# Seven products over a second group of inner tiles, in one more pair of a down projection

## The reference, cut to what matters

```python
D_MODEL = 1024
SEQ = 512
DEPTH = 2
D_FF = ((8 * D_MODEL + 3 * 256 - 1) // (3 * 256)) * 256   # 2816
...
    f = rms_norm(h, ffn_norm)
    gate, up = jnp.split(f @ w_gate_up, 2, axis=-1)
    return h + (jax.nn.silu(gate) * up) @ w_down
```

## Time and profile before

| | |
|---|---|
| median of three runs | 1248.59 us |
| profiled execution, first to last instruction | 1246.9 us |
| TensorE busy (PE) | 1232.7 us, 99% |
| VectorE busy (DVE) | 1025.6 us, 82% |
| ScalarE busy (ACT) | 699.0 us, 56% |
| GpSimd busy (POOL) | 171.2 us, 14% |
| granted TensorE clock, whole span | 1.000 |
| stretch of the down projection's pairs 1 to 3 in layer 1 | 1156.48 us to the last matmuls at about 1243.8 us |

### The profile page before, as it was taken

The page is one execution under the profiler, slowest core; times in us unless marked ns, Lnnn a source line. Parts: engine busy times, 40 slices in busy tenths (PEclk is TensorE's granted clock), DMA queues, the critical chain, the costliest instruction groups (busy, mean ns, idle before and its releaser), DMA issues.

```text
span 1246.9 us, 23723 instructions
## 1 busy us (share of the span) xinstructions
PE 1232.7 (99%) x9336; PEld 1181.9 (95%) x9336; DVE 1025.6 (82%) x1692; ACT 699.0 (56%) x1158; POOL 171.2 (14%) x120
## 2 busy tenths in 40 slices
PE   7999999999999999999999999999999999999999
PEld 7999999999999999999998899988899999998998
DVE  5797789588999999897665888894989999989865
ACT  6675547656555555753355765395665555558332
POOL 2564213100000000000033553121000000000000
PEclk9999999999999999999999999999999999999999
DMA  5322111132322222233323221110422332212333
GB/s 198 103 73 86 52 35 35 35 135 71 133 103 102 102 102 69 85 100 118 105 89 102 92 85 53 52 35 18 135 102 102 129 109 102 102 69 85 119 119 119
DMA packets 27387, 114.01 MB, mean 91 GB/s; under 512 B 3472, under 2 KB 4112, under 8 KB 21904
## 3 DMA queue, kind: packets, MB, share of 16 engines
q1 hardware_dynamic: 26560, 111.45, 26.9%
q10 hardware_dynamic: 720, 1.09, 0.2%
HBM read 108.79 MB, written 2.10 MB: 89 GB/s over the span
## 4 chain that ended last, share of the span: by engine, by line
PE 94%; DVE 3%; ACT 1%; issue 1%; POOL 1%; DMA 0%; SPq 0%; DVEq 0%; ACTq 0%; POOLq 0%
PE ps L1404 22%; PE ps L1410 11%; PE ps L1019 11%; PE ps L1115 6%; PE ps L1121 6%; PE ps L1116 6%; PE ps L1025 5%; PE ps L1488 5%; PE ps L1524 4%; PE ps L1245 3%; PE ps L1493 2%; PE ps L1529 2%; PE ps L1193 2%; PE ps L1218 2%; PE ps L1228 1%
## 5 line engine op out<-in xcount | busy, mean ns | idle before, releaser
L1115 PE MATMUL ps<-xhi,whi 128*128 128x264 f32 (+1 forms) x616 | 174.0, 310 | 1.3 <-DVE feat L2251 1.3
L1116 PE MATMUL ps<-xlo,whi 128*128 128x264 f32 (+1 forms) x616 | 167.5, 300 | 0.0
L888 POOL TENSOR_TENSOR wlo<-raw,whi 128x1024 fp32r<-128x1024 f32 x48 | 119.1, 2483 | 181.6 <-ACT whi L1702 181.0
L1115 PEld LDWEIGHTS ps<-xhi,whi 128*128 128x128 f32 x616 | 116.1, 188 | 5.9 <-DVE feat L2251 1.5
L1116 PEld LDWEIGHTS ps<-xlo,whi 128*128 128x128 f32 x616 | 116.2, 189 | 3.6
L1702 ACT ACTIVATE whi<-raw 128x1024 fp32r<-128x1024 f32 x74 | 77.9, 1054 | 55.0 <-PE ps L1025 30.6
L1121 PE MATMUL ps<-xhi,wlo 128*128 128x264 f32 (+1 forms) x616 | 100.5, 305 | 0.8 <-POOL wlo L888 0.8
L1121 PEld LDWEIGHTS ps<-xhi,wlo 128*128 128x128 f32 x616 | 85.3, 188 | 5.1 <-POOL wlo L888 1.2
L1404 PE MATMUL ps<-fhi,hi_a 128*128 128x264 f32 (+1 forms) x352 | 88.2, 283 | 0.0
L1404 PE MATMUL ps<-flo,hi_a 128*128 128x264 f32 (+1 forms) x352 | 88.1, 282 | 0.0
L1404 PE MATMUL ps<-flo,hi_b 128*128 128x264 f32 (+1 forms) x320 | 80.3, 283 | 0.0
(11 more groups left out here) (376 smaller groups left out, 3871.9 us busy)
## 6 DMA issues: line engine op xcount, KB each, us to landing
raw<-in_weights SPq DMA_DIRECT2D x116, 512.0 KB, 3.5
raw<-in_groups SPq DMA_DIRECT2D x42, 1024.0 KB, 4.8
out_hT<-h SPq DMA_DIRECT2D x7, 256.0 KB, 4.9
h<-in_hT SPq DMA_DIRECT2D x4, 264.0 KB, 6.3
h<-in_hT ACTq DMA_DIRECT2D x4, 264.0 KB, 6.0
cst<-in_consts SPq DMA_DIRECT2D x1, 780.5 KB, 9.0
xnb<-feat SPq DMA_DIRECT2D x10, 66.5 KB, 2.1
feat<-xnb SPq DMA_DIRECT2D x10, 66.5 KB, 2.1
```

The source lines that it names most:

```text
L888: nc.gpsimd.tensor_tensor(wlo[:, b], raw[:, b], whi[:, b].bitcast(F32), ALU.subtract).then_inc(split_done, 1)
L1115: nc.tensor.matmul(o, whi[:, k % 2, n], xhi[:, n, cut], start=(n == 0), stop=False)
L1116: nc.tensor.matmul(o, whi[:, k % 2, n], xlo[:, n, cut], start=False, stop=False)
```

## The change

The table gets pair 1 of layer 1, and VectorE makes the low parts of the second forms earlier in that pair, since they are now read there. Pair 1 of layer 0 stays with one group. The host lays the weights of pair 1 out in the other order of units.

```diff
-DN_TWO = ((2, 3), (2, 3))
+DN_TWO = ((2, 3), (1, 2, 3))
...
                             split_down(v + 2)
                             dn_second_weight_sums(p)
                             split_down(v + 3)
+                            if p == 1:
+                                dn_second_forms_low()
                             for a in range(2):
                                 dn_second_sums_low(p, a)
```

## The result

The changed kernel takes **1254.24 us** (median of five, 1253.17 to 1255.08) against 1248.59 (1248.36 to 1249.31): 5.65 us slower, ratio 1.0043 with a 95% interval of 1.0033 to 1.0054. The forecast was 1252.7. The profiled execution took 1254.38 us, its span is 1252.6 (before: 1246.9), and its mean granted clock 0.997 (before: 1.000).

What follows compares the result with a forecast made beforehand. TensorE was taken to bound the kernel, with no slack in layer 1's down projection. Saved work −0.65 plus waits 4.75 gave +4.1 us on 1248.59: 1252.7 us, range 1251.3 to 1254.5.

Steps and rivals of the forecast that it cites:

- sum_vp starts: VectorE's first weight sum in pair 1, forecast at 1162.60 us, 3.61 us later relative to TensorE than in pair 2.
- 1. first F1, high: First group's F1 high product in pair 1 waits for ScalarE's rounded sums; S 0.35 us, 0.46 with the refill.
- 2. first F1, low: First group's F1 low product in pair 1 waits for VectorE's xhi, ending at 1166.41 us; S 0.94 us.
- 3. unit 3, high: Second group's raw high product in pair 1 waits for unit 3's late load and rounding, 1169.70 us; S 2.33.
- 4. unit 3, low: Second group's raw low product in pair 1 waits for VectorE's split of unit 3, ending 1171.27 us; S 3.43.
- 5. second F1, high: Second group's F1 high product in pair 1 waits for the low second forms, ending 1173.47 us; S 4.68.
- 6. second F1, low: Second group's F1 low product in pair 1: low sums met within 0.1 us, S 4.75, nothing late afterwards.
- The term −0.65: TensorE's matmul work saved in pair 1, 66 units of 256 columns in place of 72: 0.65 us won.
- S: TensorE's accumulated delay in pair 1 against pair 2's timing, through the second group's F1 products; forecast 4.75 us.
- VectorE's lateness: VectorE in pair 1 comes 3.61 us later relative to TensorE than in pair 2, and can't catch up.
- The rival: TensorE falls to its lower clock after the waits in pair 1, adding 1.7 us: 1254.4 us; chance 8%.
- The lag stays: Rival: pair 1's snapshots or units 4 and 5 also come a microsecond late, 1253.7 us; chance 7%.

Runs made afterwards that it cites:

- e7: Changed kernel without the low second forms and the second half of the first group's low forms in layer 1 (timing only): 1249.06 us, ratio 1.0006.
- e5: Changed kernel without the low parts of the second forms in layer 1 (timing only): 1252.24 us, ratio 1.0030 to the kernel before.
- e6: Changed kernel without the second half of the first group's low forms in layer 1 (timing only): 1251.02 us, ratio 1.0019 to the kernel before.
- e3: Changed kernel with pair 1's first weight sums made ahead of the second half of the low forms: 1254.10 us, ratio 1.0043 to the kernel before.
- e9: e3 with TensorE's rests filled by 11 and 7 matmuls that nothing reads: 1251.90 us, ratio 1.0027 to the kernel before.
- e8: Changed kernel with layer 1's low second forms made on VectorE near 1144 us, not in pair 1: 1254.64 us, ratio 1.0041 to the kernel before.
- e2: Changed kernel with 22 matmuls that nothing reads ahead of TensorE's three longest waits of pair 1: 1252.57 us, ratio 1.0031 to the kernel before.
- e1: The changed kernel run again unaltered, as yardstick of its batch: 1252.96 us, ratio 1.0043 to the kernel before.
- e4: Changed kernel with layer 1's low second forms made on GpSimd in place of VectorE: 1255.39 us, ratio 1.0053 to the kernel before.
- e10: e8 with 12 and 6 matmuls that nothing reads filling two of TensorE's rests: 1252.82 us, ratio 1.0035 to the kernel before.

## Why the prediction was right, and where it was not

Times after the pair's first matmul (forecast: less 1156.32; measured: less 1155.67):

| step | forecast | measured |
|---|---|---|
| sum_vp starts | 6.28 | 6.29 |
| 1. first F1, high | 8.73 | 8.83 |
| 2. first F1, low | 10.15 | 10.15 |
| 3. unit 3, high | 13.44 | 13.50 |
| 4. unit 3, low | 15.01 | 15.08 |
| 5. second F1, high | 17.21 | 17.28 |
| 6. second F1, low | 17.81 | 18.30 |
| pair 2 starts | 33.63 | 35.90 |

**The term −0.65, TensorE's own work.** Right. e7 shows it, where pair 1 takes 29.96 us with S of 1.09: 28.87 without.

**VectorE's lateness and the waits, items 1 to 5.** Right within 0.1 us each, in order and by releaser. The method held: take a template from the same trace and move each engine by its own offset. e5, e6 and e7 show that the two blocks of low forms carry 3.5 of the 4.64 us, e3 and e9 that the load of unit 3 is worth only the 0.56 us that VectorE rests for it and a little more, and e8 that the place of the second forms is worth nothing (S 4.70 without the clock): the sum of VectorE's work ahead of the second products is what counts.

**Item 6 and the rest.** The wait was met, but the four matmuls before it ran at half the clock. This is the term that failed: the sum, −0.65 + 4.75, has no term for the clock, which stood among the rivals at 8%. The 24 matmuls from 1172.95 to 1178.18 took 5.23 us in place of 2.83. That is 2.4 us, of which 0.1 had been counted as refill. The rival had said 1.7, from a stretch of 3.69 us at the lower clock; here it lasted about 7 us, 5.23 of them behind the last wait. With it the forecast of pair 1, 33.63, becomes the 35.90 measured. What went wrong was the weighing: one rest of 1.33 us in a stretch that was otherwise busy said little about four rests close together. In the changed kernel TensorE was busy 4.32 of the 6 us from 1164 on, and 2.70 of the next 4. I wrote that this was more rest than any row had, and still gave it 8%.

The rival's time, 1254.4 from the earlier trace rows, was within 0.2 us of the median, and that closeness is luck in part: its price for the clock was 0.6 us too low, and the median grew 0.7 us less than pair 1 did in the profiled execution. e2 and e9 against e1 and e3 show that it is the rests that bring the clock down: with them filled it keeps 1.00.

The Trainium skill, "TensorE: Matmul & The Clock Gate", section "A second HAM failure mode: psum-queue depth-cycling", says that frequent short idles between groups of matmuls make the clock swing between its two levels. Here the trace agrees: the granted clock was 1.00 up to 1171 us, 0.50 from 1174 to 1178, and 1.00 behind. I had held one row of this case against it.

**The lag stays.** Out: the fix waits 5.42 us (3.2 forecast, and 2.3 of it is the clock), pairs 2 and 3 keep their length.

**The time.** The range (1251.3 to 1254.5) held it; the point was 1.5 us too low, and the forecast's own bounds, 1252.2 to 1253.2, did not hold. It was the room left for the rivals that took the median in, by 0.3 us, and one of the five executions (1255.08) lies outside. In the repeat (e1) it came to 4.09 us over before, as forecast: that agreement is luck in part, since three of its five executions lost little or nothing to the clock, and one of five in the first measurement. Both belong to one program: the waits cost about 3.7 to 4.2 us net whatever the execution, and the clock adds 0 to 2.4 by the execution. Part of it is where the fall comes. In the profiled executions of e1, e3, e4, e8 and e10 the granted clock was down for 3 to 4 us, in the changed kernel's for about 7, and in e1 most of that lay under waits that TensorE had anyway, so that about 0.5 us was lost. What decides when it falls and for how long was not found out, only that filled rests take it away.

No order tried beats the kernel before. The most that the seven products can win here is 0.65 us, and even with 4.4 us of VectorE's work left out altogether pair 1 was still 0.43 us longer.

## What to carry to other kernels

Fewer matmuls are a gain only where the engine that prepares their operands is early: lay the same form, where the kernel already runs it, over the new place, with one offset for each engine, and look at what each wait has as margin. When the result is that a saturated TensorE gets several rests close together, put a price on its clock as well, even if every rest is short. And before moving work from VectorE to GpSimd, look for what VectorE runs at the same time: here one VectorE instruction took 4.86 us beside GpSimd's, in place of 1.23.

## What the runs showed of the hardware that was not expected

- Rests of 0.24, about 0.15, 1.19, 0.84 and 0.55 us, the first ending at 1164.5 and the last at 1172.95, went with a fall of the granted clock from 1.00 to 0.50 (matmuls of 256 columns 0.215 us apart in place of 0.118) from about 1171.3 to 1178.2 us. It fell while TensorE was working, between two rests. With rests of 0.84 and 1.00 us alone (e6) the clock stayed in the profiled execution and fell in two of eleven (0.998); with 0.24, 1.17 and 0.84 us (e5) it stayed in the profiled one and fell in four of seven; with 0.79 us alone (e7) it fell in none of eleven. In e10 one rest of 1.56 us, ending at 1165.65 us, and one of about 0.15 us at 1166.98 were all that stood ahead of a fall at about 1167.4.
- The same program loses between nothing and 2.4 us this way, and the changed kernel's executions form two groups 2.3 us apart, the upper at a mean clock of 0.997 (e1). A median of five can stand in either: 1252.96 and 1254.24 for one kernel.
- A GpSimd instruction of 128 by 2048 float32 elements took 4.68 us, and a VectorE subtraction that started 0.9 us after it took 4.86 us in place of 1.23.
